# Neighbourhood attention in blocks of grid column halves: 160 keys in reach of a query block in place of 256

## The reference, cut to what matters

```python
col_start = clip(c - 8, 0, 48)
in_win = (c2 >= col_start) & (c2 < col_start + 16)
s = q @ k.T * 64 ** -0.5 + where(in_win, rpb[head, dr, dc], -1e30)
o = softmax(s) @ v
```

## Time and profile before

| | before |
|---|---|
| median of three runs | 2303.09 us (2302.27 to 2304.15) |
| the profiled execution's own time | 2302.8 us |
| its span | 2301.1 us |
| PE busy | 2293.1 us |
| DVE busy | 1495.8 us (65%) |
| ACT busy | 1315.9 us (57%) |
| POOL busy | 64.8 us |
| TensorE clock granted | full in all 40 slices |

### The profile page before, as it was taken

One profiled execution on the slowest core, in us unless ns is written; L12 is line 12 of the kernel. 1 busy time (PEld: TensorE's weight loads), 2 busy tenths in 40 slices (PEclk: granted clock), 3 DMA queues, 4 the chain that ended last, 5 costly groups with the idle time before them and its releaser, 6 DMA issues.

```text
span 2301.1 us, 32405 instructions
## 1 busy us (share of the span) xinstructions
PE 2293.1 (100%) x11767; PEld 1921.9 (84%) x11767; DVE 1495.8 (65%) x2102; ACT 1315.9 (57%) x1998; POOL 64.8 (3%) x94
## 2 busy tenths in 40 slices
PE   9999999999999999999999999999999999999999
PEld 8887778888888888888888888888887888888887
DVE  5657555555577775477776677787977665555554
ACT  5457564444565554355555577667674556666653
POOL 0011100000100000000000001010000000000000
PEclk9999999999999999999999999999999999999999
DMA  8689996767766656566566756575855788977974
GB/s 270 222 253 268 265 247 211 225 203 226 241 190 195 193 185 202 171 210 192 183 187 204 241 164 193 170 210 171 229 148 175 224 250 233 259 214 239 260 227 164
DMA packets 416529, 489.61 MB, mean 213 GB/s; under 512 B 146160, under 2 KB 242320, under 8 KB 416272
## 3 DMA queue, kind: packets, MB, share of 16 engines
q1 hardware_dynamic: 409984, 479.33, 69.2%
q10 hardware_dynamic: 6416, 8.56, 1.1%
HBM read 429.07 MB, written 35.41 MB: 202 GB/s over the span
## 4 chain that ended last, share of the span: by engine, by line
PE 95%; DVE 2%; ACT 1%; DMA 1%; DVEq 0%; issue 0%; ACTq 0%; SPq 0%
PE gemm L789 23%; PE gemm L790 22%; PE gemm L791 22%; PE gemm L777 7%; PE aux L777 6%; PE gemm L769 4%; PE aux L769 3%; DVE w_lo L733 1%; PE aux L791 1%; PE aux L789 1%; PE aux L790 1%; DMA raw<-in_w_up 1%; ACT w_hi L723 1%; PE aux L2653 0%; PE aux L2849 0%; PE aux L2835 0%
## 5 line engine op out<-in xcount | busy, mean ns | idle before, releaser
L733 DVE TENSOR_TENSOR w_lo<-raw,w_hi 128x1024 fp32r<-128x1024 f32 (+1 forms) x800 | 956.6, 1207 | 582.6 <-ACT w_hi L723 579.1
L723 ACT ACTIVATE w_hi<-raw 128x1024 fp32r<-128x1024 f32 (+1 forms) x800 | 813.0, 1041 | 468.4 <-PE gemm L791 290.4
L789 PE MATMUL gemm<-w_lo,hT 128*128 128x512 f32 x1600 | 632.7, 395 | 0.6 <-DVE w_lo L733 0.3
L791 PE MATMUL gemm<-w_hi,hT 128*128 128x512 f32 x1600 | 623.4, 390 | 0.0
L790 PE MATMUL gemm<-w_hi,hT 128*128 128x512 f32 x1600 | 623.4, 390 | 0.0
L789 PEld LDWEIGHTS gemm<-w_lo,hT 128*128 128x128 f32 x1600 | 300.5, 188 | 67.5 <-issue 4.5
L791 PEld LDWEIGHTS gemm<-w_hi,hT 128*128 128x128 f32 x1600 | 300.4, 188 | 63.0
L790 PEld LDWEIGHTS gemm<-w_hi,hT 128*128 128x128 f32 x1600 | 300.6, 188 | 59.7 <-issue 0.2
L777 PE MATMUL gemm<-hT,w_hi 128*128 128x512 f32 x704 | 216.7, 392 | 0.4 <-DVE w_lo L733 0.4
L777 PE MATMUL aux<-hT,w_hi 128*128 128x512 f32 x672 | 207.6, 390 | 0.0
L789 PE MATMUL gemm<-w_lo,yT_hi 128*128 128x512 f32 x472 | 184.1, 390 | 0.0
(11 more groups left out here) (346 smaller groups left out, 2190.7 us busy)
## 6 DMA issues: line engine op xcount, KB each, us to landing
raw<-in_w_up SPq DMA_DIRECT2D x336, 256.0 KB, 2.9
raw<-in_w_in SPq DMA_DIRECT2D x144, 512.0 KB, 4.8
raw<-in_a_w_in SPq DMA_DIRECT2D x128, 512.0 KB, 3.9
raw<-in_b_w_in SPq DMA_DIRECT2D x128, 512.0 KB, 4.5
raw<-in_w_down SPq DMA_DIRECT2D x76, 512.0 KB, 4.6
raw<-in_w_branch SPq DMA_DIRECT2D x32, 512.0 KB, 5.1
raw<-in_w_out SPq DMA_DIRECT2D x32, 512.0 KB, 4.9
raw<-in_a_w_out SPq DMA_DIRECT2D x32, 512.0 KB, 4.2
```

The costliest lines, as they stand in the source:

```text
L723: nc.scalar.activation(hi, src, ACT.Copy).then_inc(S("hi_done"), 1)
L733: nc.vector.tensor_tensor(lo, src, hi.bitcast(F32), ALU.subtract).then_inc(S("lo_done"), 1)
L789: nc.tensor.matmul(dst, xh, wl[:, k, :], start=h["start"] and k == 0, stop=False)
L791: mm = nc.tensor.matmul(dst, xl, wh[:, k, :], start=False, stop=h["stop"] and k == h["n"] - 1)
```

## The change

Tokens are regrouped by column halves. Queries are kept in DRAM in column-major order (token = 4 * column + row, `keep_by_column`), so that query block `tb` holds one column half, and values are written to `va` by column half (`quarters`). Keys stay in token order, and `scores` reads 40 of each grid row's 64 columns. What changes on each engine:

- PE: each `scores` product has 160 key columns in place of 256 (as many products). Each unit's `values` have, for each head, products of 160, 64 and 96 query columns in place of two of 256: 6 products in place of 4.
- DVE: `masked` works on 320 elements in place of 512, in the bias's own buffer; `scaled_rows` has 8 multiplications in place of 4 (4 of 128 and 4 of 32 elements, the latter 8 columns of each of 4 rows), and for the first two units 4 `memset`s of 128 elements, which set the far parts of the probability buffers to 0 once; `low` is 2 instructions of 256 elements in place of one of 512, its input read in another order. The wait for the planes of unit u - 2 moves from `masked` to `scaled_rows`.
- ACT: exponentials of 160 in place of 256 elements; `high` in 2 instructions; the word splitting is unchanged (the far parts, 0, are split and turned as well).
- ACT and DVE: the evacuation of v (tiles 6 and 9) is 4 instructions of 32 partitions each in place of one of 128.
- POOL: each of the 32 mask instructions has 128 partitions of 192 elements in place of 64 of 576.
- DMA: the skewed copies are 32 of 320 elements for each head in place of 64 of 896; each bias load has 128 rows of 640 bytes in place of 384 of 256 bytes (u of 4 and above now wait for `na_scaled` in place of `na_max`); three small DMAs near the start lay the table out in DRAM (`na_rows`), on which ACT's first copy and, with the gains, the later waits for `gains_landed` wait; each keep of queries is 2 DMAs in place of one.

The core of the diff:

```diff
 NAH, NAD = 16, 64
 NAW = NAH * NAD
 NKR, NKC, GRID = 8, 16, 64
-SPAN = 6
+ROWS = T // GRID
+HALF = GRID // 2
+SEEN = HALF + NKC // 2
+KEYS = ROWS * SEEN
...
+
+                sp.wait_ge(S("planes"), i + 1)
+                rows_ = row_planes[slot].rearrange("(c r) w e -> r c (w e)", r=ROWS)
+                for tb in range(TB):
+                    sp.dma_start(rows_[2 * tb:2 * tb + 2], src[:, tb, :, :].rearrange("p w c -> p (w c)")).then_inc(S(event), 16)
...
             def load_bias(u, j):
-                a, h = j // 2, j % 2
+                tb, h = j // 2, j % 2
                 sp.wait_ge(S(f"na_copied{u // 2}"), 16)
                 if u >= BR:
-                    sp.wait_ge(S("na_max"), 2 * (u - BR) + 2)
-                src = bass.AP(tensor=na_skew.tensor, offset=(2 * u + h) * GRID * SKEW + (1 - a) * P + GRID - 1,
-                              ap=[[SKEW - 1, GRID], [P, SPAN], [1, GRID]])
-                sp.dma_start(bias[a * GRID:(a + 1) * GRID, u % BR, h, :, :], src).then_inc(S(f"bias_landed{u % BR}"), 16)
+                    sp.wait_ge(S("na_scaled"), u - BR + 1)
+                src = bass.AP(tensor=na_skew.tensor, offset=(2 * u + h) * HALF * SKEW + ROWS * SEEN - NKC // 2 * tb,
+                              ap=[[SKEW - 1, HALF], [-SEEN, ROWS], [1, KEYS]])
+                sp.dma_start(bias[:, u % BR, tb, h, :], src).then_inc(S(f"bias_landed{u % BR}"), 16)
...
+            for cols, src in ((slice(edge, SKEW - edge), rpb[:, :, GRID - 1 - edge:GRID - 1 + edge]),
+                              (slice(0, edge), rpb[:, 0, 0:edge]), (slice(SKEW - edge, SKEW), rpb[:, 0, 0:edge])):
+                dst = na_rows[:, cols].rearrange("h (k c) -> h k c", c=SEEN) if cols.start == edge else na_rows[:, cols]
+                sp.dma_start(dst, src).then_inc(S("gains_landed"), 16)
             sp.dma_start(lng[:, :], ins["gm_ln_g"][0].partition_broadcast(P)).then_inc(S("consts_landed"), 16)
...
                         for tb in range(TB):
-                            part = sc[u % 2][:, tb, a * T:(a + 1) * T]
+                            part = bias[:, u % BR, tb, a, :]
                             e = A(part, part, ACT.Exp, bias=mx[:, at, tb:tb + 1], accum_out=sm[:, at, tb:tb + 1])
                         e.then_inc(S("na_exp"), 1)
...
-                    A((va[g] if part == 2 else qkv_tok)[:, 0, :], G[t % 2][0][:, :], ACT.Copy,
-                      scale=rstd[:, 0, 0:1]).then_inc(S("read_out0"), 1)
+                    if part == 2:
+                        for to, half_, own_ in quarters(0):
+                            e = A(va[g][to, half_, :], G[t % 2][0][own_, :], ACT.Copy, scale=rstd[own_, 0, 0:1])
+                        e.then_inc(S("read_out0"), 1)
+                    else:
+                        A(qkv_tok[:, 0, :], G[t % 2][0][:, :], ACT.Copy, scale=rstd[:, 0, 0:1]).then_inc(S("read_out0"), 1)
...
             def attend():
                 def masked(u):
                     dve.wait_ge(S("bias_masked"), 2 * u + 2)
-                    if u >= 2:
-                        dve.wait_ge(S("planes"), NA_TURNS[u - 2] + 1)
                     for a in range(2):
                         dve.wait_ge(S("na_scores"), 2 * u + a + 1)
-                        b0 = bias[:, u % BR, a, 2, 0:1]
-                        window = bass.AP(tensor=b0.tensor, offset=b0.offset,
-                                         ap=[list(b0.ap[0]), [-2 * GRID, TB], [1, T]])
-                        part, at = sc[u % 2][:, :, a * T:(a + 1) * T], u % 2 * 2 + a
-                        V.scalar_tensor_tensor(out=part, in0=score_banks(u % 2)[a][:, :].rearrange("p (t k) -> p t k", t=TB),
-                                               scalar=float(NAD) ** -0.5, in1=window, op0=ALU.mult, op1=ALU.add)
+                        part, at = bias[:, u % BR, :, a, :], u % 2 * 2 + a
+                        V.scalar_tensor_tensor(out=part, in0=score_banks(u % 2)[a][:, :].rearrange("p (t k) -> p t k", t=TB)[:, :, 0:KEYS],
+                                               scalar=float(NAD) ** -0.5, in1=part, op0=ALU.mult, op1=ALU.add)
                         dve.drain()
                         V.tensor_reduce(mx[:, at, :], part, AX_X, ALU.max)
                         dve.drain()
                         V.tensor_scalar(mx[:, at, :], mx[:, at, :], -1.0, None, ALU.mult).then_inc(S("na_max"), 1)
                 def scaled_rows(u):
+                    far = [sc[u % 2][:, tb, a * T + (1 - tb) * P:a * T + (2 - tb) * P] for a in range(2) for tb in range(TB)]
+                    if u < 2:
+                        for part in far:
+                            V.memset(part, 0.0)
+                    else:
+                        dve.wait_ge(S("planes"), NA_TURNS[u - 2] + 1)
                     dve.wait_ge(S("na_exp"), 2 * u + 2)
                     both = slice(u % 2 * 2, u % 2 * 2 + 2)
                     V.reciprocal(ri[:, both, :], sm[:, both, :])
                     dve.drain()
                     for a in range(2):
                         for tb in range(TB):
-                            part = sc[u % 2][:, tb, a * T:(a + 1) * T]
-                            e = V.tensor_scalar(part, part, ri[:, u % 2 * 2 + a, tb:tb + 1], None, ALU.mult)
+                            part = bias[:, u % BR, tb, a, :].rearrange("p (r c) -> p r c", r=ROWS)
+                            own_half = sc[u % 2][:, tb, a * T + tb * P:a * T + (tb + 1) * P].rearrange("p (r c) -> p r c", r=ROWS)
+                            other = far[a * TB + tb].rearrange("p (r c) -> p r c", r=ROWS)
+                            f = ri[:, u % 2 * 2 + a, tb:tb + 1]
+                            edge = SEEN - HALF
+                            V.tensor_scalar(own_half, part[:, :, tb * edge:tb * edge + HALF], f, None, ALU.mult)
+                            e = V.tensor_scalar(other[:, :, (HALF - edge) * tb:(HALF - edge) * tb + edge],
+                                                part[:, :, HALF * (1 - tb):HALF * (1 - tb) + edge], f, None, ALU.mult)
                     e.then_inc(S("na_scaled"), 1)
                 def low(n):
                     dve.wait_ge(S("yb_hi"), n + 1)
-                    at = slice(8 + 2 * n, 10 + 2 * n)
-                    V.tensor_tensor(yT_lo[:, at, :], AX[0][:, :].rearrange("p (u t) -> p u t", u=2), yT_hi[:, at, :].bitcast(F32),
-                                    ALU.subtract).then_inc(S("yb_lo"), 1)
+                    for i in range(2):
+                        e = V.tensor_tensor(yT_lo[:, 8 + 2 * n + i, :].rearrange("p (r c) -> p r c", r=ROWS),
+                                            AX[0][:, i * T:(i + 1) * T].rearrange("p (c r) -> p r c", r=ROWS),
+                                            yT_hi[:, 8 + 2 * n + i, :].bitcast(F32).rearrange("p (r c) -> p r c", r=ROWS), ALU.subtract)
...
                         for tb in range(TB):
                             for a in range(2):
                                 rows_ = slice(a * NAD, (a + 1) * NAD)
-                                m = MM(score_banks(u % 2)[a][:, tb * T:(tb + 1) * T], qT[rows_, u % 4, tb * P:(tb + 1) * P],
-                                       kT[rows_, u % 4, :], start=True, stop=True)
+                                near = slice(tb * (GRID - SEEN), tb * (GRID - SEEN) + SEEN)
+                                m = MM(score_banks(u % 2)[a][:, tb * T:tb * T + KEYS], qT[rows_, u % 4, tb * P:(tb + 1) * P],
+                                       kT[rows_, u % 4, :].rearrange("p (r c) -> p r c", r=ROWS)[:, :, near], start=True, stop=True)
                                 if tb:
                                     m.then_inc(S("na_scores"), 1)
                         pe.wait_ge(S("yb_lo"), n)
                     pe.wait_ge(S(f"na_turned{n % 2}"), 32 * (n // 2 + 1))
                     for u in (2 * n, 2 * n + 1):
-                        for kb in range(TB):
+                        for kb, to, first in ((0, slice(0, KEYS), True), (1, slice(T - KEYS, KEYS), False), (1, slice(KEYS, T), True)):
                             for a in range(2):
                                 h = 2 * (u % 4) + a
-                                m = MM(AX[0][a * NAD:(a + 1) * NAD, u % 2 * T:(u % 2 + 1) * T], va[n // 2][:, kb, h * NAD:(h + 1) * NAD],
-                                       pT_of(u)[:, 2 * a + kb, :], start=kb == 0, stop=kb == TB - 1)
+                                m = MM(AX[0][a * NAD:(a + 1) * NAD, u % 2 * T + to.start:u % 2 * T + to.stop],
+                                       va[n // 2][:, kb, h * NAD:(h + 1) * NAD], pT_of(u)[:, 2 * a + kb, to], start=first, stop=kb == 1)
```

More of the change, by code:

```diff
@@ L106, in written @@
 def written(i):
-    return i - 8
+    return i - 7
 def turned(i):
@@ L224, in program @@
         BR = 4
-        r = Region(scratch - 2 * nbytes([P, 2, SPAN, GRID]))
-        bias = r.put("bias", [P, BR, 2, SPAN, GRID])
+        r = Region(scratch - 2 * nbytes([P, 2, 6, GRID]))
+        bias = r.put("scores", [P, BR, TB, 2, KEYS])
```

(36 more changed lines are left out.)

47 lines of the change are left out of this document (30 added, 17 removed).

## The result

Against the kernel before in the same rounds (2303.35 us), the changed kernel takes 2306.48 us (median of 20 runs, 2303.59 to 2310.11): a ratio of 1.0013, 95% interval 1.0007 to 1.0019. That is 3.1 us or 0.13% more, within the 0.2% that the prediction called no change, and outside its range. The profiled execution took 2307.34 us with a span of 2305.3, 4.2 more than before.

The account below looks back on a forecast made before the run. PE was taken as the bound, busy 2293.1 of 2301.1 us. Gains of 2.55 + 2.45 + 0.8 + 0.2 = 6.0 us off 2302.8 gave 2296.8, plus 0.3 for the median: 2297.1 us, range 2295.5 to 2300.6.

Parts of the forecast that it names:

- What lies under cover: Side work on DVE, ACT, POOL and the DMA queues: mostly 0 us; the queries' keep in two DMAs 0, at worst 0.5.
- PE, scores and values: Narrower products in the attention's four scores and four values groups on PE: 2.55 us and 2.45 us gained.
- Rival 1: Weight loads pace PE's narrow pairs in scores and values groups: 2.8 us gained in all, 2300.3 us; 12%.
- Late halves: Halves whose w_lo comes late, 200 to 345 us: 1.1 us gained, 0.3 lost behind scaled rows, 0.8 us net.
- one more: A third late half, besides those at 217 and 300 us, expected on time; the three together 1.1 us.
- masked and scaled rows: For each unit on DVE: masked and maxima 0.68 us less, eight multiplications 1.6 us, 0.4 more; ACT's exponentials 0.07 less each.
- rival 3: Scaled rows become the bound at the half behind each of eight: 2306 us at the outside, priced 2305; 7%.
- Rival 2: Half of PE's 5.0 us returns as waits for DMA, DVE and ACT: 2.5 to 3.5 gained, 2300.0 us; 12%.
- v, high, low, memsets, POOL: Extra instructions for v, high, low and memsets, and POOL's smaller masks: 0 us; v up to 2 if cover is gone.
- The skewed copies: Four copies shrinking from 896 to 160 KB beside the weight loads: 0.2 us gained, between 0 and 0.5.
- a sign of chance: A change of more than 0.5 us outside 125 to 345 us would make the forecast right or wrong by chance.

Follow-up runs that it names:

- the base: The changed kernel with each keep of queries in four DMAs of 64 token rows in place of two (the keep spread): 2297.77 us, 2297.94 when run again.
- the test with four: The kernel with the keep spread, with the four small multiplications of each unit's scaled rows left out: 2295.72 us, ratio 0.9969.

## Why the prediction was wrong

It forecast 2297.1 us and 0.26% less; measured was 0.13% more. By its own steps:

- **The step that failed** is in "What lies under cover": "The keep of queries in two DMAs occupies SP's queue for one more issue, twice ... 0, at worst 0.5." It priced the issue and not the transfer. Measured: 8.7 us (2306.5 against 2297.8), because each DMA lay on 2 engines. Without that cost, the forecast of 2297.1 stands against 2297.8 and 2297.9 measured for the kernel with the keep spread; the 0.7 to 0.8 us that are left are the term for late halves, below. The `2` stands in front of the destination in the diff; the prediction did not look at it. By the rates measured the term comes out large enough: 256 KB at 50 GB/s is 5.2 us for each DMA, 10.5 for a keep (5.1 us lie between the events of the two, 212.8 and 217.9), in a stream whose raw loads are issued 10 to 15 us ahead of their use (halves 86 to 93 of the base).
- **PE, scores and values**: 2.55 and 2.45 us forecast; from the signals 4 x 0.64 = 2.56 and 4 x 0.62 = 2.47. Right. The four pairs more of a values group cost what was taken for them, almost nothing.
- **Rival 1**, the weight loads as the pace, is refuted by the same numbers (it had 1.8 us in all). The reading of the Trainium skill's page "TensorE: Matmul & The Clock Gate", section "The mechanism", by which a values group would lose 0.2 us in uncovered loads is not borne out: 1.26 us was forecast without it and measured.
- **Late halves**: those of 217 and 300 us (halves 72 and 99) were to be on time, and with the keep spread they are: 0.32 + 0.59 = 0.91 us. The "one more" that was to make it 1.1 was half 91 or 92, and these got worse; half 48, at 147 us and outside the places counted, is on time too, 0.16. Against it 0.3 was set for new late halves; halves 90 to 92 lost 0.97 in that kernel. With half 48 that is 0.1 net in place of 0.8, and apart from the keep this term was furthest off.
- **masked and scaled rows**: an operation of 320 elements takes 0.485 us where 512 took 0.685, four of them 0.80 us less for each unit (0.68 forecast); exponentials 417 ns against 500, 0.08 each (0.07); the eight multiplications 1.46 us from the first's start to the last's end in six of the eight units and up to 1.84 in the others (1.6), beside 1.14 before. All near the forecast, and rival 3, which needed 2.4 us, did not come as priced; but the growth of 0.3 us for each unit does cost time at halves 90 to 92, as the test with four shows.
- **Rival 2**, PE's gain taken back as waits, is true in part: widening the values or the scores brought only 1.0 to 1.9 of 2.5 us back. About 1 us of PE's 5.0 is lost to it at halves 90 to 92, and moving two keeps recovers it.
- **v, high, low, memsets, POOL** cost nothing that shows; v's was tested by itself. The skewed copies were 0.2: half 16, 2.85 us before, is at 2.72, its `w_lo` ready 4.6 us ahead of PE where it was 0.3: 0.13 us. Half 48's 0.16 is of the same kind. Both are put down to the copies by the four late events of each load, and not tested by themselves. The prediction had no row for a load that was late for a copy, so that its 0.2 came out near is luck.
- **Elsewhere**: up to the start of half 42, at 131 us, the kernel after is 0.5 us slower than before, and behind half 118, at some 360 us, 0.45 faster. So no change of more than 0.5 us shows outside the attention, which the prediction had named as a sign of chance.

Of half 72's 7.43 us the idle time is 5.1. The rest is the clock: the granted clock fell from 1.00 to 0.50 (1.2 GHz, the lower of its two levels) at 220.6 us, after PE had stood still from 217.2 on, and was back at 227.4; 12 products at 0.43 us in place of 0.23 are 2.4 us.

Left open are whether the skewed copy alone blocked SP's queue for 6.4 us in the kernel before with the narrow keep, why halves 80 and 81 were that late beside the first keep, where the 0.3 to 0.7 us come from that the four multiplications gave beyond halves 90 to 92, and why half 19, before the attention, takes 0.15 us more than before.

## What to carry to other kernels

When a change rewrites a DMA's access pattern, read the outermost dimension on both sides before its bytes: here 2 in place of 128 cost 8.7 us of a kernel whose PE had gained 5.0, while four DMAs of 64 rows carry the same bytes at no cost that shows. Such a DMA harms what is issued behind it, on the same queue (half 72) and, as the loads beside ACT's skewed copies suggest, on another one; so look for its victims in the loads that follow and not in its own consumer. The sign in a trace is a load whose last few semaphore events come microseconds after the rest. And where a stream is just in time, price PE's gain against the transfers beside it: they don't get faster, and moving one that isn't urgent may give more back than the compute that was saved.

## What was not expected of the hardware

- With a DMA of outermost dimension 2 in front, the whole set of engines fell to 48 to 51 GB/s at a share of 0.13 to 0.15 (217 to 220 us), though weight loads of 512 KB were queued behind it: two of 16 engines held up the whole stream. Of the load of half 72, 14 of 16 semaphore events were there by 213.8 us, the last at 219.8; the load behind it had none before 221.1.
- The lower clock came late and stayed past the wait: PE's last product before half 72 ended at 217.2 us, the clock fell at 220.6, PE went on at 222.3 and ran some 5 us of products at 0.50, up to 227.4. In the kernel before with the narrow keep the longest wait was 7.8 us, up to 155.4, and the clock was at 0.50 from 150.8 to 161.1.
- A multiplication of 32 elements (4 rows of 8) in a row of such takes 0.15 us up to the next one's start, where its own duration is 0.23.
